# Transposing the hidden tiles after they are split in two parts, instead of before

## The reference

```python
hid = jnp.square(jax.nn.relu(x @ w_mlp1[l]))              # mlp: 1024 -> 4096 -> 1024
x = layer_norm(ALPHA * x + hid @ w_mlp2[l], ...)

def swiglu(x, w_in, w_out):                               # ffa, ffb, ffc, ffd
    gate, up = jnp.split(x @ w_in, 2, axis=-1)            # 1024 -> 2 x 2816 -> 1024
    return (jax.nn.silu(gate) * up) @ w_out

def mixer_b(...):                                         # mixb: 1024 -> 3072 -> 1024
    z = jax.nn.gelu(h @ w_in + b_in)
    u, v = jnp.split(z, 2, axis=-1)
    ...                                                   # v: layer norm, 128-token mixing
    return (u * sv) @ w_out
```

## Time and profile before

| | |
|---|---|
| Median of 3 runs | 1436.81 us (1434.79 to 1441.68) |
| The profiled execution's own time | 1436.81 us |
| Its span, first to last instruction | 1435.1 us |
| PE busy | 1398.9 us |
| DVE busy | 824.7 us |
| ACT busy | 601.5 us |
| Hidden groups transposed (count of L515) | 144 |
| Transposes of L1282 | 288 |

### The profile page before, as it was taken

How to read it: one execution, slowest core, us unless ns; L and a number is a source line. 1 busy time by engine, 2 the same in 40 slices (tenths; PEclk the granted TensorE clock), 3 DMA queues, 4 the chain that set the end, 5 groups by cost and what they waited for, 6 DMA issues and landing times.

```text
span 1435.1 us, 17631 instructions
## 1 busy us (share of the span) xinstructions
PE 1398.9 (97%) x6732; PEld 1163.1 (81%) x6732; DVE 824.7 (57%) x847; ACT 601.5 (42%) x662; POOL 56.2 (4%) x84
## 2 busy tenths in 40 slices
PE   6999999999999999999999999999999999999997
PEld 6877788877888889878888888888887888888886
DVE  6437654566444556776544474445667775654452
ACT  5432443435334442336344353444453343544431
POOL 1001000011000000002000010000001000100000
PEclk9889999999999989999999999999999999999999
DMA  8513745437454454245555445544463745355540
GB/s 336 211 60 135 263 164 214 175 118 279 178 195 183 175 182 170 79 161 217 181 202 201 178 184 191 196 175 176 176 247 142 271 184 212 146 214 201 201 147 29
DMA packets 38966, 263.64 MB, mean 184 GB/s; under 512 B 4489, under 2 KB 4497, under 8 KB 9089
## 3 DMA queue, kind: packets, MB, share of 16 engines
q1 hardware_dynamic: 34272, 245.38, 45.9%
q0 software_dynamic: 4640, 17.50, 3.6%
HBM read 261.81 MB, written 2.63 MB: 184 GB/s over the span
## 4 chain that ended last, share of the span: by engine, by line
PE 90%; DVE 5%; ACT 2%; DMA 1%; issue 1%; POOL 1%; DVEq 0%; POOLq 0%; SPq 0%; ACTq 0%
PE mm L1154 19%; PE mm L1156 19%; PE mm L1155 19%; PE acc L1154 9%; PE acc L1156 9%; PE acc L1155 9%; PE tp L1282 2%; DVE wlo L706 2%; DMA raw<-slabs_dram 1%; PE acc L1475 1%; ACT whi L475 1%; PE tp L1250 1%; PE mm L1587 1%; PE mm L1387 1%; DVE h L772 0%
## 5 line engine op out<-in xcount | busy, mean ns | idle before, releaser
L706 DVE TENSOR_TENSOR wlo<-raw,whi 128x2048 fp32r<-128x2048 f32 x232 | 524.3, 2288 | 140.5 <-ACT whi L475 140.4
L475 ACT ACTIVATE whi<-raw 128x2048 fp32r<-128x2048 f32 x232 | 436.8, 1915 | 53.6 <-DMA raw<-slabs_dram 47.3
L1154 PE MATMUL mm<-whi,xt 128*128 128x512 f32 (+1 forms) x1104 | 432.8, 392 | 15.3 <-DVE wlo L706 11.5
L1156 PE MATMUL mm<-whi,xt 128*128 128x512 f32 (+1 forms) x1104 | 430.8, 390 | 0.0
L1155 PE MATMUL mm<-wlo,xt 128*128 128x512 f32 (+1 forms) x1104 | 430.4, 390 | 0.0
L1154 PEld LDWEIGHTS mm<-whi,xt 128*128 128x128 f32 x1104 | 209.4, 190 | 58.5 <-issue 11.5
L1156 PEld LDWEIGHTS mm<-whi,xt 128*128 128x128 f32 x1104 | 209.3, 190 | 43.2
L1155 PEld LDWEIGHTS mm<-wlo,xt 128*128 128x128 f32 x1104 | 209.4, 190 | 42.3
L1154 PE MATMUL acc<-whi,ht 128*128 128x512 f32 x576 | 234.4, 407 | 1.7 <-DVE wlo L706 1.7
L1156 PE MATMUL acc<-whi,ht 128*128 128x512 f32 x576 | 225.5, 392 | 0.0
L1155 PE MATMUL acc<-wlo,ht 128*128 128x512 f32 x576 | 225.0, 391 | 0.0
(11 more groups left out here) (141 smaller groups left out, 874.7 us busy)
## 6 DMA issues: line engine op xcount, KB each, us to landing
raw<-slabs_dram SPq DMA_DIRECT2D x232, 1024.0 KB, 4.9
vec<-vectors_dram POOLq DMA_DIRECT2D x23, 512.0 KB, 5.7
tables_dram<-table_dram POOLq DMA_DIRECT2D x1, 1536.0 KB, 10.8
hlf<-x_turned_dram SPq DMA_DIRECT2D x2, 512.0 KB, 5.4
h<-x_dram POOLq DMA_DIRECT2D x2, 512.0 KB, 4.6
htf<-tables_dram POOLq DMA_DIRECT2D x1, 1024.0 KB, 7.9
h<-bands_dram POOLq DMA_DIRECT2D x1, 768.0 KB, 9.3
reg<-w_sp_dram POOLq DMA_DIRECT2D x1, 512.0 KB, 8.1
```

The lines of the kernel that those rows point to most:

```text
L475: nc.scalar.activation(whi[:, m % RING, :], raw[:, m % RAW, :], ACT.Copy).then_inc(hi_done, 1)
L706: nc.vector.tensor_tensor(wlo[:, m % RING, :], raw[:, m % RAW, :], whi[:, m % RING, :], ALU.subtract).then_inc(lo_done, 1)
L1154: nc.tensor.matmul(out, a[0], b[0], start=first, stop=False)
L1156: return nc.tensor.matmul(out, a[1], b[0], start=False, stop=last)
```

## The change

The hidden tile is now split into its two parts before it is transposed. After `unit`, ACT copies `hid` to the high part `hl[:, t, 0]` (`hidden_hi`), and DVE writes `hid` minus the high part to `hl[:, t, 1]` (`hidden_lo`). PE transposes both parts as float32r, with a float32r identity `idr`, into the four quarters of a bank of `tp`, so there are four transposes in a group where there were two. `turned` is on ACT alone and copies all 512 columns of a group to `ht`, high and low part together. DVE's `turned` is gone. PE's `turn` waits for `hl_ready` (DVE's low part) where it waited for `hid_ready`, and a bank of `tp` is free after ACT's copy. The buffer `hid` is free once `hl` is written, so the gates no longer wait for the transposes. `hl` lies in memory that the fused stages did not use.

```diff
             def fused(stg, f, gate, width):                      # ACT
 
+                def hidden_hi(c, t, i):
+                    act.wait_ge(stg.hid_ready, 2 * c + t + 1 + i * 2 * f.period)
+                    if c > 0:
+
+                        act.wait_ge(stg.tp_ready, f.rows * (2 * c + t - 1) + i * 2 * f.rows * f.period)
+                    nc.scalar.activation(hl[:, t, 0, 0:width], hid[:, t * N:t * N + width], ACT.Copy)\
+                      .then_inc(stg.hl_hi, 1)
+
                 def turned(c, t, i, place=None):
...
-                        nc.scalar.activation(ht[:, place, 0, 2 * j:2 * j + 2, :],
-                                             tp[:, g % 2, 0:SEQ].rearrange("p (q n) -> p q n", q=2),
-                                             ACT.Copy).then_inc(stg.ht_hi, 1)
+                        nc.scalar.activation(ht[:, place, :, 2 * j:2 * j + 2, :],
+                                             tp[:, g % 2, :].rearrange("p (i q n) -> p i q n", i=2, q=2),
+                                             ACT.Copy).then_inc(stg.ht_ready, 1)
...
                     gate(c, 0, i)
                     turned(c - 1, 1, i)
+                    hidden_hi(c, 0, i)
                     hi(m + f.s - 1, f, i)
                     gate(c, 1, i)
                     turned(c, 0, i)
+                    hidden_hi(c, 1, i)
...
             def silu_gate(stg, f, n):
...
-                    else:
-
-                        act.wait_ge(stg.tp_ready, 2 * c + t - 1 + i * 2 * f.period)
...
             def relu_gate(c, t, i):
                 unit_done(act, mlp, f_mlp, c, t, i)
                 if c > 0:
-                    act.wait_ge(mlp.tp_ready, 2 * (2 * c + t - 1) + i * 4 * f_mlp.period)
+                    act.wait_ge(mlp.hl_ready, 2 * c + t - 1 + i * 2 * f_mlp.period)
...
             def fused(stg, f, unit, width):                      # DVE
 
-                def turned(c, t, i, place=None):
...
+                def hidden_lo(c, t, i):
+                    dve.wait_ge(stg.hl_hi, 2 * c + t + 1 + i * 2 * f.period)
+                    nc.vector.tensor_tensor(hl[:, t, 1, 0:width], hid[:, t * N:t * N + width],
+                                            hl[:, t, 0, 0:width], ALU.subtract).then_inc(stg.hl_ready, 1)
...
                     unit(c, 0, i)
-                    turned(c - 1, 1, i)
+                    hidden_lo(c, 0, i)
                     lo(m + f.s - 1, f, i)
                     unit(c, 1, i)
-                    turned(c, 0, i)
+                    hidden_lo(c, 1, i)
...
                 def turn(c, t, i):                               # PE
-                    pe.wait_ge(stg.hid_ready, 2 * c + t + 1 + i * 2 * f.period)
+                    pe.wait_ge(stg.hl_ready, 2 * c + t + 1 + i * 2 * f.period)
...
-                        for q in range(2):
-                            ins = nc.tensor.transpose(
-                                tp[:, g % 2, q * P:(q + 1) * P],
-                                hid[:, t * N + (2 * j + q) * P:t * N + (2 * j + q + 1) * P], idf[:, :])
+                        for part in range(2):
+                            for q in range(2):
+                                ins = nc.tensor.transpose(
+                                    tp[:, g % 2, (2 * part + q) * P:(2 * part + q + 1) * P].bitcast(F32R),
+                                    hl[:, t, part, (2 * j + q) * P:(2 * j + q + 1) * P], idr[:, :])
                         ins.then_inc(stg.tp_ready, 1)
```

## The result

The changed kernel takes 1460.15 us (median of 4 runs, 1458.79 to 1461.89) against 1438.14 us of the kernel before beside it: ratio 1.0163, 95% interval 1.0142 to 1.0183, thus 22 us slower. I had forecast 1469 us, 32 us slower, with 1462 as the lower end. The sign and the place were right; the price of one transpose was not, and the time lies just under the range.

The account below looks back on a forecast made before the run. PE was taken to bound the fused stages: 1436.8 + 32.1 (new transposes) - 0.9 (start of mlp) + 1.1 (stage ends) = 1469.1, so 1469 us, 2.2% slower; range 1462 to 1492.

Parts of the forecast that it names:

- What bounds the kernel: In the six fused stages PE is always busy, so work added to PE counts in full; PE busy 97% overall.
- The price of a float32 transpose: In mlp, four transposes between `up` and `down` matmuls cost PE 0.1115 us each; the 288 cost 32.1 us.
- The new transposes: In the fused stages, 576 float32r transposes replace 288 float32 ones at 0.1115 us each: +32.1 us on PE.
- the nearest row: Float32r matmul of 8 columns, 0.11 us after the one before; taken as the cost of a new 128-column stationary block.
- The bounds of 0.06 and 0.16: Per float32r transpose: 0.06 us if only columns counted (+2.5 us), 0.16 from 128-column, 8-row matmuls (+60).
- DVE and ACT: Within chunks, DVE's load about unchanged and ACT's extra copies fit beside PE's work: priced at nothing.
- Start of mlp: Eight new transposes come before PE's 1.70 us wait for a late slab and vanish in it: -0.9 us.
- Stage ends: At the ends of ffa, ffb and ffc PE waits longer for the norm, 0.4 more at ffa: +1.1 us together.
- Rival 1: Float32r transposes dearer than float32 ones: 0.16 us each gives 1497 us, 0.21 gives 1526; chance 0.08.
- Rival 2: In `turn`, float32r transposes cheap, doubled count free: from 0.056 us each, not slower; 1439.5 us at 0.06; chance 0.08.
- Rival 3: At the ends of ffa, ffb and ffc waits grow and the clock falls: 5 us more, 1474 us; chance 0.10.

Follow-up runs that it names:

- float32 half loads: Kernel before with 288 more float32 transposes, each of only the first 64 columns of the same blocks: 1469.26 us, ratio 1.0213.
- product with the identity: Changed kernel with its 576 float32r transposes replaced by ordinary float32r products with the identity, transpose mode off: 1472.08 us, ratio 1.0233 to the kernel before.
- the one with the high part only: Changed kernel without the low part's transposes, ACT's copy reading the high part twice: 1437.05 us, ratio 0.9999 to the kernel before.

## Why the prediction was wrong

- **What bounds the kernel**: right. PE is full in the chunks of both kernels, and 83.5 us more on ACT cost nothing there: 142.76 us for the 17 blocks of ffb with the split ahead or behind.
- **The price of a float32 transpose**, 0.1115 us: right, and confirmed by the changed kernel in float32 (+36 us, +33 at one clock) and by the float32 half loads at 0.106 us.
- **The new transposes**: this is the term that was mis-sized. "I take 0.1115: 576 x 0.1115 = 64.2, which is +32.1 us." Measured 0.366 us for a block of four and 0.716 for eight, together 52.3 for the 576, 0.091 each, and 19.9 more than before (20.7 over whole chunks). ffa, which was to be 4.9 us longer, has 22 blocks at 0.16, 3.5 us. The step from the nearest row failed: it took a stationary load of 128 columns to cost the same in a product as in a transpose. The product with the identity shows the 0.113 that I had assumed, and the transpose mode shows 0.09. The agreement of two rows at 0.11 made this look firmer than it was; the records of the weight loads, 139 ns against 190, spoke against it and I did not use them. The bounds of 0.06 and 0.16 did hold it, but my range went down to 1462 only, which is 0.099 a transpose, and so left out everything from there to 0.06. It is chance that the time missed by no more than 2 us.
- **DVE and ACT**: right as to cost within the chunks, with the copies at 418 ns where I took 0.38 us and ACT's waits at a silu gate down to 3.7 us (323.9 / 88) from 4.3.
- **Start of mlp**: -0.9 forecast, -0.5 measured. **Stage ends**: +1.1 forecast, +1.4 measured, with the wait after ffa at 1.3 us for the 1.2 that I gave. Some 1 to 2 us of the earlier split are in neither term.
- **Rival 1** (dearer) is excluded. **Rival 2** (half price) had the right direction from the forecast but not the size: it needed 0.056. The rule of the Trainium skill beside it, "TensorE: Matmul & The Clock Gate", section "Weight-path perf modes — Fast Weight Load (FWL) and DoubleRow", ties the fast load to the number of weights and the type. An ordinary float32r product with 128 weights costs 0.113 us here, no less than a float32 transpose, and what makes the difference in the runs is the transpose mode: the record of the load is 139 to 141 ns in the transposes of either type and 190 in the product. Whether the fast load was on in either is shown by no run. **Rival 3** (clock) did not come: the changed kernel's 11 executions have a mean granted clock of 0.982 to 0.989, and those of the kernel before 0.982 to 0.988. The six microseconds after the longer wait at ffa had clock 1.00 in the profiled execution, but that alone shows little, since the changed kernel with float32 transposes and the one with the high part only each have a stretch at 0.50 just behind this wait (520.5 to 523.5 us and 514.5 to 517.5). The blocks of eight in mlp stand in a stretch (150 to 320 us) at granted clock 1.00 throughout, so the rule of the Trainium skill, same page, section "Part 4: PE-mode transpose", that transposes don't count as PE being busy left no mark.

## What to carry to other kernels

Where an engine is full, count its slots from starts, not from the lengths of records, and take the slot from the same form of instruction: a transpose and a product of one type and size are not one price. When two unlike rows agree on a number, ask what bounds each before lending it to a third; a lower end of a range belongs at the lower bound while that is open. And a transpose can be tried under the cheaper type before anything is rebuilt around it. Where an effect is a few microseconds, compare executions at the same granted clock: here that took 2 us from one gain and added 3 to another.

## What the runs showed that I had not expected

- The output stays right when plain float32 data is transposed as float32r, with all 472 blocks of the kernel done so. The split ahead of the transposes was not needed for them. That all 32 bits pass would explain it, but no run compares the bits.
- In blocks a float32r transpose costs 0.206 us for two, 0.366 for four and 0.716 for eight; that is a fixed 0.04 and 0.083 to 0.088 for each. Float32 has next to no fixed part: 0.226, 0.446, 0.886.
- With 64 in place of 128 stationary columns a float32r transpose takes 0.05 to 0.06 us, and a float32 one still 0.11.
